# Gathering u by pair and v by token: two half-size gathers in place of one, and the sum over v in 32-column products

## The chip, the core and the metric

The kernel runs on one core of a Trainium2 chip, in float32 throughout. The metric is the device time of one execution in microseconds (us), median of several runs. Five engines work side by side: PE (TensorE, matrix products), DVE (VectorE), ACT (ScalarE), POOL (GpSimd), which here issues the indirect DMAs, and SP, which issues the plain loads. 16 DMA engines move the data.

## The reference

Two blocks are computed, one after the other, on 256 tokens of width 1024; the first block also carries 256 context tokens. The change touches one part of the first block, the expert layer:

```python
def peer_ffn(x, w_q, sub_keys, u_emb, v_emb):      # chunks of 128 tokens
    q = (xc @ w_q).reshape(128, 8, 2, 128)
    s = einsum('thid,hikd->thik', q, sub_keys)
    # top 16 of each half, top 16 of their 256 sums: eidx, top_s [128, 8, 16]
    gate = softmax(top_s, axis=-1)
    u = u_emb[eidx]
    hid = gelu(einsum('td,thkd->thk', xc, u))
    wgt = gate * hid
    return einsum('thk,thkd->td', wgt, v_emb[eidx])
```

Each token has 8 heads x 16 = 128 pairs (head, rank), and each pair names one of 16,384 experts. An expert has a row of u and a row of v, 1024 floats (4 KB) each. For each pair the token's vector is multiplied with the u row and summed (the dot), the result goes through gelu and the gate, and with this weight the v row is added to the token's output. The layer runs three times: over the 256 tokens in layer 0, over the 256 context tokens in layer 0, and over the 256 tokens in layer 1.

## The kernel before

Each run of the expert layer (here a gather stage; its name in the code is `peer00`, `peer01` or `peer10`) takes two tiles of 128 tokens, with the tokens on the partitions. A tile has 8 steps, one a head, so a stage has 16 steps of 16 pairs: 256 gathers `e`.

- `peer_sp` loads the query weights and keys. `peer_pe` makes the queries and then, step by step, the scores (line 1180).
- `route_dve` turns one step's scores into 16 expert numbers and 16 gates for every token. It is a generator: `peer_dve` runs one piece of it for step+1 after each dot of step, from the third on (`next(routing, None)`), and the rest at the end of the step. The tenth piece gives the numbers and the gates.
- `peer_pool` issues one indirect DMA for each pair (line 1334). Row t of it is the expert row that token t names, from a table `uv` in which an expert's u and v rows lie side by side: 128 rows of 8 KB, about 1 MB. They land in a ring of 8 slots in `big`. At a step's end `fetched_pool` makes POOL wait until the step's last gather has landed, since the expert numbers have only two buffers.
- DVE takes the dot of the u half with the tokens' vectors, which lie in PSUM (line 1300). ACT makes gelu of the one column in four instructions (lines 1222 to 1225). DVE spreads weight times gate on the diagonal of a 128 x 128 matrix (line 1309), and PE multiplies this diagonal with the v half in two products of 512 columns, which add up in PSUM over the tile's 128 pairs (line 1200). Each such float32 product stands in the profile as two records.
- A slot comes free when PE has summed its v half. After a tile DVE multiplies the sum with the modulation row and adds it to `h` (lines 1319 and 1324).

The second stage, `peer01`, has side work: `together` weaves `ahead_pe`, `ahead_act` and `ahead_dve` between the steps. They make projections of the next layer in 8 turns, each with 2 MB and 1.5 MB of weights that SP loads when PE has finished with the buffer, and results stored by ACT's queue. The main programs say by `yield` how far they are, from 0 to 256, and each side program's pieces come due as a share of that.

## Time and profile before

| | |
|---|---|
| runs, median (lowest to highest) | 4519.16 us (4517.67 to 4519.98) |
| profiled execution: time / span | 4520.76 us / 4519.5 us |
| PE busy / DVE busy / ACT busy / POOL busy | 3599.4 / 2209.3 / 1248.7 / 834.0 us |
| indirect gathers | 768, 805.36 MB in all |
| mean granted TensorE clock | 0.918 of full speed |

The span is the time from the first to the last instruction of the profiled execution, and the views of the trace count microseconds from its start. Busy time is the time in which an engine worked; it says nothing of what held the kernel up. For that one reads which wait ended last in each stage.

### The profile page before, as it was taken

To read this page: it belongs to the slowest core of one execution; us is meant where nothing else is said; L and a number is where in the kernel's file an instruction comes from. 1 tells how busy PE (TensorE), PEld (TensorE's weight loads), DVE (VectorE), ACT (ScalarE), POOL (GpSimd) and SP (SyncE) were. 2 spreads that over 40 slices of the span, in tenths; PEclk is the share of its full clock that TensorE was granted. 3 is DMA by queue.
4 is the path that set the end of the run, shared out by engine and by line. 5 is a ranking of instruction groups with operands and counts; after the bars stand their busy time and mean duration, and the time that the engine had idled before them with its cause. 6 is when DMAs were issued, how large, how long until landed. Compare 5 with 4: busy or idle time off the path is not lost.

```text
span 4519.5 us, 30080 instructions
## 1 busy us (share of the span) xinstructions
PE 3599.4 (80%) x9346; PEld 1688.1 (37%) x9346; DVE 2209.3 (49%) x4937; ACT 1248.7 (28%) x3913; POOL 834.0 (18%) x872
## 2 busy tenths in 40 slices
PE   7799998878777777679898897777777777787786
PEld 1144444544422222254444443343522222234343
DVE  0101520462577777536777775333377777622132
ACT  0010000331244444324444442021244444411111
POOL 0000100000233333213233332000133333300000
PEclk9899999989999999889999998988899899998898
DMA  7712222022689898869999997212689898942322
GB/s 268 264 56 75 56 75 79 21 75 74 274 363 384 361 382 364 341 224 385 401 401 389 404 392 271 93 63 94 238 365 384 362 382 363 380 157 75 115 80 93
DMA packets 283753, 1087.17 MB, mean 241 GB/s; under 512 B 17180, under 2 KB 73500, under 8 KB 184256
## 3 DMA queue, kind: packets, MB, share of 16 engines
q0 software_dynamic: 110592, 805.36, 43.7%
q1 hardware_dynamic: 169672, 274.65, 17.6%
q10 hardware_dynamic: 3328, 5.24, 0.3%
q8 instruction: 73, 1.20, 0.1%
q14 instruction: 88, 0.72, 0.0%
HBM read 1078.79 MB, written 6.40 MB: 240 GB/s over the span
## 4 chain that ended last, share of the span: by engine, by line
PE 52%; DMA 29%; DVE 11%; issue 3%; POOL 2%; ACT 1%; SPq 1%; DVEq 0%; POOLq 0%; ACTq 0%
DMA big<-in_uv,smallu 22%; PE ps L221 18%; PE ps L1200 13%; PE ps L477 6%; PE ps L415 4%; PE ps L1168 3%; DVE tmp L1300 3%; DMA w<-in_w_in 2%; DMA w<-in_w_mod 2%; PE ps L1069 2%; PE ps L489 2%; DMA w<-in_peer_wq 2%; POOL big L1334 2%; DVE xT L1309 1%; PE ps L1078 1%
## 5 line engine op out<-in xcount | busy, mean ns | idle before, releaser
L1200 PE MATMUL ps<-big,xT 128*128 128x512 f32 x3072 | 1534.3, 637 | 441.0 <-DVE xT L1309 439.6
L1300 DVE CUSTOM_DVE_ANT_0 tmp<-big,ps 128x1024 f32<-128x1024 f32 x768 | 934.5, 1217 | 507.8 <-DMA big<-in_uv,smallu 504.9
L1200 PEld LDWEIGHTS ps<-big,xT 128*128 128x128 f32 x3072 | 582.1, 200 | 1302.9 <-DVE xT L1309 770.7
L1334 POOL DMA_INDIRECT big<-in_uv,smallu x768 | 727.7, 948 | 1646.0 <-PE ps L1200 1097.7
L221 PE MATMUL ps<-w,xT 128*128 128x512 f32 x1600 | 697.6, 598 | 31.7 <-DMA w<-in_w_in 26.4
L1222 ACT ACTIVATE xT<-xT 128x1 f32<-128x1 f32 x768 | 155.7, 203 | 1163.3 <-DVE xT L1300 1156.2
L221 PEld LDWEIGHTS ps<-w,xT 128*128 128x128 f32 x1600 | 306.2, 192 | 418.1 <-issue 410.7
L1309 DVE TENSOR_SCALAR xT<-ident,xT 128x128 f32<-128x128 f32 x768 | 274.6, 363 | 140.0 <-ACT xT L1225 140.0
L1225 ACT ACTIVATE xT<-xT 128x1 f32<-128x1 f32 x768 | 297.2, 387 | 25.7
L477 PE MATMUL ps<-w,xT 128*128 128x512 f32 x576 | 259.1, 612 | 54.4 <-DMA w<-in_w_in 53.2
L1224 ACT ACTIVATE xT<-xT 128x1 f32<-128x1 f32 x768 | 226.1, 294 | 25.1
L1223 ACT ACTIVATE xT<-xT,small 128x1 f32<-128x1 f32 x768 | 226.1, 294 | 24.9
L1168 PE MATMUL ps<-tmp,w 128*128 128x256 f32 x768 | 178.6, 396 | 39.8 <-DMA w<-in_peer_wq 37.7
L221 PE MATMUL ps<-w,small 128*2 128x512 f32 x384 | 169.1, 597 | 31.9 <-DMA w<-in_w_mod 31.0
L477 PEld LDWEIGHTS ps<-w,xT 128*128 128x128 f32 x576 | 112.5, 197 | 197.8 <-issue 189.3
L1168 PEld LDWEIGHTS ps<-tmp,w 128*128 128x128 f32 x768 | 152.8, 200 | 64.4 <-DMA w<-in_peer_wq 38.9
L415 PE MATMUL ps<-xT,w 128*128 128x512 f32 x384 | 165.1, 592 | 0.7 <-ACT big L393 0.7
L231 PE MATMUL ps<-ident,merged 128*128 128x128 f32 x208 | 43.0, 395 | 122.4 <-DVE merged L282 49.3
L1069 PE MATMUL ps<-w,merged 128*128 128x512 f32 x256 | 130.2, 617 | 5.4 <-DVE tmp L1121 4.9
L518 DVE TENSOR_SCALAR tmp<-tmp 128x512 f32<-128x512 f32 x36 | 15.4, 427 | 235.4 <-ACT tmp L508 233.6
L253 ACT ACTIVATE tmp<-h 128x1024 f32<-128x1024 f32 x22 | 23.2, 1056 | 383.6 <-DVE big L332 199.2
L366 POOL TENSOR_TENSOR small<-small 128x32 f32<-128x32 f32 x8 | 43.3, 5415 | 464.2 <-DVE small L356 464.2
(207 smaller groups left out, 2610.2 us busy)
## 6 DMA issues: line engine op xcount, KB each, us to landing
w<-in_w_in SPq DMA_DIRECT2D x48, 2048.0 KB
w<-in_w_mod SPq DMA_DIRECT2D x24, 2048.0 KB
w<-in_w_in SPq DMA_DIRECT2D x48, 512.0 KB
w<-in_peer_wq SPq DMA_DIRECT2D x12, 2048.0 KB
w<-in_w_out SPq DMA_DIRECT2D x8, 2048.0 KB
big<-in_uv,smallu POOLq DMA_INDIRECT x768
bc<-mods SPq DMA_DIRECT2D x20, 512.0 KB, 7.0
w<-in_conv_out_w SPq DMA_DIRECT2D x4, 2048.0 KB
```

The costliest lines, as they stand in the source:

```text
L221: ins = pe.e.matmul(self.ps[0:rows, b, :], lhs(k, tile), self.wk(s, kc)[:, k, :], start=k == 0, stop=k == kc - 1)
L415: ins = pe.e.matmul(self.ps[:, 3 * s + g, 0:n], view[:, k, g, :], self.xT[:, k, 0:n], start=k == 0, stop=k == KC - 1)
L477: ins = pe.e.matmul(self.ps[:, self.gate_bank(n, product, c, i), :], self.lhs(k, tile), self.wk(s)[:, k, :], start=k == 0, stop=k == KC - 1)
L1069: ins = pe.e.matmul(self.ps[:, 6 + i, :], xT[:, k, i * P:(i + 1) * P], proj_w[:, k, :], start=k == 0, stop=k == KC - 1)
L1168: ins = pe.e.matmul(self.ps[:, 5 + i % 3, 0:256], self.wk(c % 2)[:, k, g * P:(g + 1) * P], p["xT"][:, k, :], start=k == 0, stop=k == KC - 1)
L1200: ins = pe.e.matmul(self.ps[:, 2 + half, :], p["diag"][:, e % RING, :], p["ring"][:, e % RING, D + half * BANK:D + (half + 1) * BANK], sta ...
L1223: act.inc(act.x.activation(g1, g1, ACT.Identity, scale=0.044715 * ROOT, bias=self.root_2_pi))
L1224: act.inc(act.x.activation(g2, g1, ACT.Tanh, scale=x))
L1225: act.inc(act.x.activation(wt, g2, ACT.Identity, scale=x, bias=x), name, "gelu", e)
L1300: dve.inc(dve.e.tensor_tensor_reduce(out=p["junk"][k % 2], in0=p["ring"][:, e % RING, 0:D], in1=p["xc"], scale=1.0, scalar=0.0, op0=ALU.mu ...
L1309: dve.inc(dve.e.tensor_scalar(p["diag"][:, e % RING, :], self.ident[:, :], p["wt"][u][:, c:c + 1], p["gates"][u][:, c:c + 1], ALU.mult, AL ...
L1334: ins = pool.e.indirect_dma_start(p["ring"][:, e % RING, :], None, self.d["uv"], bass.IndirectOffsetOnAxis(p["eidx"][step % 2][:, k:k + 1] ...
```

## The change

The table `uv` is split in two, `u` and `v`. A gather fetches 128 rows of 4 KB of one table, so a stage has 512 of them, each half as large. The ring in the same memory has 16 slots of half the size.

For u, a gather still belongs to one pair, with the tokens on the partitions. For v it belongs to one token, with that token's 128 pairs on the partitions: the expert numbers of a tile are turned on PE (`turn_experts`) and copied to `eidxT`. So v of a tile can be fetched only when all 8 steps of it are routed, and summed only when all 128 dots of it are done. `peer_order` sets one order for all engines: the 128 u gathers of tile 0; then v of tile 0 and u of tile 1 in turn; then the 128 v gathers of tile 1. They are called parts A, B and C here.

Gelu is made once a tile on 128 x 128 values: five instructions on DVE and one tanh on ACT (`gelu_dve`). PE turns the weights, and DVE writes them with stride 33 into two zeroed buffers of 2048 columns (`diag_dve`). Token 32j+m has there a block of 128 x 32 in which only column m is filled. Its product with the token's v rows adds the weighted sum of the 128 pairs to row m of the PSUM partitions 32j to 32j+31. Four tokens, one of each j, are taken in a group: 8 products of 512 columns. The numbers and gates of a whole tile are kept, so that `fetched_pool` is gone. A u slot comes free with its dot, a v slot with its group's products.

```diff
-RING, LAG = 8, 2
+RING, LAG = 16, 2
...
+    def peer_order(self):
+        order = [("u", e) for e in range(P)]
+        for i in range(P):
+            order += [("v", i), ("u", P + i)]
+        return order + [("v", P + i) for i in range(P)]
...
     def peer_pe(self, pe, l, stream):
...
-                pe.wait_ge(self.dve, name, "spread", e)
-                for half in range(2):
-                    ins = pe.e.matmul(self.ps[:, 2 + half, :], p["diag"][:, e % RING, :], p["ring"][:, e % RING, D + half * BANK:D + (half + 1) * BANK],
...
+            if n == 0:
+                turn_weights(tile)
+                pe.wait_ge(self.dve, name, "diag", tile)
+                if tile:
+                    pe.wait_ge(self.dve, name, "summed", 0)
+            if n % 4 == 3:
+                m, slots = n // 4, [self.v_slot[e - 3 + j] for j in range(4)]
                 for half in range(2):
+                    for j in range(4):
+                        if not half:
+                            pe.wait_ge(self.gathered[slots[j]], name, "v", e - 3 + j)
+                        ins = pe.e.matmul(self.ps[32 * j:32 * j + 32, 2 + half, :], p["diag"][j // 2][:, (j % 2) * D + 32 * m:(j % 2) * D + 32 * m + 32],
+                                          p["ring"][:, slots[j], half * BANK:(half + 1) * BANK], start=m == 0, stop=m == 31)
+                pe.inc(ins, name, "sum", e // 4)
...
     def route_dve(self, dve, l, name, p, step):
...
-        if step >= 2:
-            dve.wait_ge(self.pool, name, "fetched", step - 2)
-        dve.inc(dve.x.tensor_tensor(p["eidx"][u], row[:, 0:16], row[:, 16:32], ALU.add), name, "experts", step)
+        dve.inc(dve.x.tensor_tensor(p["eidxf"][tile][:, cols], row[:, 0:16], row[:, 16:32], ALU.add))
+        dve.inc(dve.x.tensor_copy(p["eidx"][tile][:, cols], p["eidxf"][tile][:, cols]), name, "experts", step)
...
+    def gelu_dve(self, dve, name, p, tile):
+
+        x, g1, g2 = p["hid"][tile], p["g1"], p["g2"]
+        dve.inc(dve.x.tensor_tensor(g1, x, x, ALU.mult))
+        dve.inc(dve.x.tensor_scalar(g1, g1, 0.044715 * ROOT, ROOT, ALU.mult, ALU.add))
+        dve.inc(dve.x.tensor_tensor(g1, g1, x, ALU.mult), name, "inner", tile)
+        dve.inc(dve.x.tensor_tensor(x, x, p["gates"][tile], ALU.mult))
+        dve.wait_ge(self.act, name, "tanh", tile)
+        dve.inc(dve.x.scalar_tensor_tensor(out=g2, in0=g2, scalar=1.0, in1=x, op0=ALU.add, op1=ALU.mult), name, "weights", tile)
...
     def peer_dve(self, dve, l, stream, ahead=False):
...
+            slot = self.u_slot[e]
+            dve.wait_ge(self.gathered[slot], name, "u", e)
...
+            dve.inc(dve.e.tensor_tensor_reduce(out=row, in0=row, in1=p["xc"], scale=1.0, scalar=0.0, op0=ALU.mult, op1=ALU.add,
+                                               accum_out=p["hid"][tile][:, e % P:e % P + 1]), name, "dot", e)
+            if k >= LAG:
+                next(routing, None)
+            if e % P == P - 1:
+                alone(routing)
+                self.gelu_dve(dve, name, p, tile)
+                self.diag_dve(dve, name, p, tile)
+                if tile:
+                    self.summed_dve(dve, name, p, 0, self.h[:, 2 * stream, :])
...
     def peer_pool(self, pool, l, stream):
...
+        for at, (kind, e) in enumerate(order):
+            tile, n, slot = e // P, e % P, at % RING
+            if at >= RING:
+                before, b = order[at - RING]
+                if before == "u":
+                    pool.wait_ge(self.dve, name, "dot", b)
+                else:
+                    pool.wait_ge(self.pe, name, "sum", b // 4)
+            if kind == "u":
+                if e % TOPK == 0:
+                    pool.wait_ge(self.dve, name, "experts", e // TOPK)
...
+                if n == 0:
+                    pool.wait_ge(self.dve, name, "eidxT", tile)
...
-    def fetched_pool(self, pool, name, step):
-
-        pool.wait_ge(self.gathered[(step * TOPK + TOPK - 1) % RING], name, "row", step * TOPK + TOPK - 1)
-        pool.inc(pool.e.nop(), name, "fetched", step)
...
-        together(self.peer_pe(pe, 0, 1), [(0, 256, self.ahead_pe(pe.beside()))])
+        together(self.peer_pe(pe, 0, 1), [(0, 512, self.ahead_pe(pe.beside()))])
```

The side work of the second stage is spread over the 512 places of the new order, a quarter of it over part A.

What stands on the engines changes as follows. On POOL, at the start of the first gather stage of the kernel before (`waits` names the counters that an instruction waits for; `gathered7` is the landing of ring slot 7):

```order
L1334 DMA big<-in_uv,smallu 128x2048 [waits dve_ops]
L1334 DMA big<-in_uv,smallu 128x2048 x7
L1334 DMA big<-in_uv,smallu 128x2048 [waits pe_ops] x8
L1334 DMA big<-in_uv,smallu 128x2048 [waits gathered7,pe_ops,dve_ops]
L1334 DMA big<-in_uv,smallu 128x2048 [waits pe_ops] x15
```

In the changed kernel POOL has at the end of part A and the start of part B of that stage (line 1392 is the new issue):

```order
L1392 DMA big<-in_u,xT 128x1024 x11
L1392 DMA big<-in_u,xT 128x1024 [waits dve_ops] x4
L1392 DMA big<-in_v,xT 128x1024 [waits dve_ops]
L1392 DMA big<-in_u,xT 128x1024 [waits dve_ops]
L1392 DMA big<-in_v,xT 128x1024
```

The wait for a landing is gone from POOL; in part A it waits for DVE alone, and the first u of tile 1 waits for numbers of the ninth step. Further on in part B:

```order
L1392 DMA big<-in_v,xT 128x1024 [waits pe_ops]
L1392 DMA big<-in_u,xT 128x1024 [waits dve_ops]
L1392 DMA big<-in_v,xT 128x1024
L1392 DMA big<-in_u,xT 128x1024 [waits dve_ops]
L1392 DMA big<-in_v,xT 128x1024
L1392 DMA big<-in_u,xT 128x1024 [waits dve_ops]
```

Here POOL waits for PE once in four v gathers, where before it waited for every slot. On DVE, the kernel before has in the middle of the first stage dots (ISA, line 1300, with the read of the accumulator behind) and spreads in turn:

```order
L1300 ISA tmp,xT<-big,ps 128x1024 [waits gathered5]
L1300 ISA xT 128x1
L1309 TENSOR_SCALAR xT<-ident,xT 128x128 [waits pe_ops]
L1300 ISA tmp,xT<-big,ps 128x1024 [waits dve_ops,gathered6]
```

In the changed kernel DVE has at the end of part A, behind the last dots of tile 0 (line 1360):

```order
L1360 ISA big,xT<-big,ps 128x1024 [waits gathered14]
L1360 ISA xT 128x1
L1360 ISA big,xT<-big,ps 128x1024 [waits gathered15]
L1360 ISA xT 128x1
L1303 TENSOR_TENSOR xT<-xT 128x128 [waits dve_ops]
L1304 TENSOR_SCALAR xT<-xT 128x128 [waits dve_ops]
L1305 TENSOR_TENSOR xT<-xT 128x128 [waits dve_ops]
L1306 TENSOR_TENSOR xT<-xT 128x128 [waits dve_ops]
L1308 SCALAR_TENSOR_TENSOR xT<-xT 128x128 [waits dve_ops,act_ops]
L1316 COPY tmp<-ps 128x2x32 [waits dve_ops,pe_ops]
L1316 COPY bc<-ps 128x2x32 [waits dve_ops]
L1348 COPY ps<-merged 128x512 [waits dve_ops] x2
```

The spreads are gone from between the dots, and the gelu of the tile stands in one piece between the tiles. On PE, the kernel before has at the start of the first stage's sums:

```order
L1200 MATMUL ps<-big,xT 128x512 [waits dve_ops]
L1200 MATMUL ps<-big,xT 128x512
L1200 MATMUL ps<-big,xT 128x512 [waits dve_ops]
```

The changed kernel has there, at the start of part B (1199 turns the expert numbers, 1203 the weights, 1194 makes scores):

```order
L1199 MATMUL ps<-ident,xT 128x128 [waits dve_ops]
L1194 MATMUL ps<-bc,bb 128x128 [waits dve_ops]
L1194 MATMUL ps<-bc,bb 128x128
L1203 MATMUL ps<-ident,xT 128x128 [waits dve_ops]
L1194 MATMUL ps<-bc,bb 128x128 [waits dve_ops]
L1194 MATMUL ps<-bc,bb 128x128
L1230 MATMUL ps<-big,tmp 32x512 [waits gathered0]
L1230 MATMUL ps<-big,tmp 32x512 [waits gathered2]
L1230 MATMUL ps<-big,bc 32x512 [waits gathered4]
L1230 MATMUL ps<-big,bc 32x512 [waits gathered6]
L1230 MATMUL ps<-big,tmp 32x512 x2
L1230 MATMUL ps<-big,bc 32x512 x2
```

The sums no longer wait for DVE, but for the landings of a group's four tokens, and each product fills 32 rows of the result.

## Rows read from the trace of the kernel before

**Rows 1.** Page, chain that ended last, by line.

```profile
DMA big<-in_uv,smallu 22%; PE ps L221 18%; PE ps L1200 13%; PE ps L477 6%; PE ps L415 4%; PE ps L1168 3%; DVE tmp L1300 3%; DMA w<-in_w_in 2%; DMA w<-in_w_mod 2%; PE ps L1069 2%; PE ps L489 2%; DMA w<-in_peer_wq 2%; POOL big L1334 2%; DVE xT L1309 1%; PE ps L1078 1%
```

**Rows 2.** Windows: stretch, its length, engines' busy us (instructions), PEclk, DMA share, GB/s.

```profile
1188.00:1900.00 712.00, 523.73 (x1080) 201.13 (x1080) 521.11 (x1324) 305.27 (x1053) 235.03 (x248) 0.92 0.90 366
2014.00:2766.00 752.00, 676.18 (x1714) 328.99 (x1712) 535.78 (x1362) 312.10 (x1067) 233.98 (x248) 0.96 0.98 388
3253.00:3965.00 712.00, 526.32 (x1080) 201.93 (x1080) 521.99 (x1325) 305.23 (x1052) 235.76 (x248) 0.92 0.90 366
5.00:200.00 195.00, 168.10 (x383) 31.29 (x384) 15.62 (x23) 0.00 (x0) 0.00 (x0) 1.00 0.75 268
```

**Rows 3.** Timeline: PE and DVE where the first gather stage begins and ends.

```profile
1187.03 0.61 PE L1180 MATMUL ps<-bc,bb 128*128 128x128 f32 x4
1899.90 1.42 DVE L1319 TENSOR_TENSOR tmp<-ps,bc 128x512 f32<-128x512 f32 x2 [4.08 <-PE ps L1200]
```

**Rows 4.** Groups by line, 1255 to 1900 us: busy us, mean ns | idle before.

```profile
L1200 PE MATMUL ps<-big,xT 128*128 128x512 f32 x920 | 465.5, 646 | 172.5 <-DVE xT L1309 172.2
L1300 DVE CUSTOM_DVE_ANT_0 tmp<-big,ps 128x1024 f32<-128x1024 f32 x228 | 277.5, 1218 | 145.4 <-DMA big<-in_uv,smallu 145.0
L1334 POOL DMA_INDIRECT big<-in_uv,smallu x224 | 212.0, 946 | 420.5 <-PE ps L1200 239.9 <-DMA big<-in_uv,smallu 152.4 <-issue 27.6
L1309 DVE TENSOR_SCALAR xT<-ident,xT 128x128 f32<-128x128 f32 x230 | 82.1, 363 | 11.4 <-ACT xT L1225 11.4
```

**Rows 5.** Waits, 1255 to 1900 us: total us, times, longest us.

```profile
POOL big L1334 <- DMA big<-in_uv,smallu: 152.4, 14, 12.3
```

**Rows 6.** Timeline: POOL at a step's start; first gather and first dot.

```profile
1397.06 0.94 POOL L1334 DMA_INDIRECT big<-in_uv,smallu  x1 [10.79 <-DMA big<-in_uv,smallu]
1398.30 0.94 POOL L1334 DMA_INDIRECT big<-in_uv,smallu  x1 [0.30 <-issue]
...
3205.42 1.05 POOL L1334 DMA_INDIRECT big<-in_uv,smallu  x1 [34.27 <-DVE xT L1276]
3211.03 1.22 DVE L1300 CUSTOM_DVE_ANT_0 tmp<-big,ps 128x1024 f32<-128x1024 f32 x1 [3.91 <-DMA big<-in_uv,smallu]
```

**Rows 7.** Timeline: DVE in the middle of a step, successive dots.

```profile
1233.00 1.22 DVE L1300 CUSTOM_DVE_ANT_0 tmp<-big,ps 128x1024 f32<-128x1024 f32 x1 [0.26 <-DMA big<-in_uv,smallu]
...
1237.98 1.22 DVE L1300 CUSTOM_DVE_ANT_0 tmp<-big,ps 128x1024 f32<-128x1024 f32 x1 [0.25 <-DMA big<-in_uv,smallu]
...
1240.46 1.22 DVE L1300 CUSTOM_DVE_ANT_0 tmp<-big,ps 128x1024 f32<-128x1024 f32 x1 [0.32 <-DMA big<-in_uv,smallu]
```

**Rows 8.** Timeline: DVE where thirteen gathers had already landed.

```profile
1189.27 0.30 DVE L1235 MAX8 xT<-ps 128x8 f32<-128x128 f32 x1
...
1212.25 1.21 DVE L1300 CUSTOM_DVE_ANT_0 tmp<-big,ps 128x1024 f32<-128x1024 f32 x1
1213.39 0.34 DVE L1309 TENSOR_SCALAR xT<-ident,xT 128x128 f32<-128x128 f32 x1
1213.65 1.21 DVE L1300 CUSTOM_DVE_ANT_0 tmp<-big,ps 128x1024 f32<-128x1024 f32 x1
...
1217.59 0.60 DVE L1309 TENSOR_SCALAR xT<-ident,xT 128x128 f32<-128x128 f32 x2
```

**Rows 9.** Timeline: PE, products of 64 rows, then of 128 rows.

```profile
860.62 1.13 PE L638 MATMUL ps<-w 64*128 64x512 f32 x4
...
883.08 2.85 PE L638 MATMUL ps<-w 64*128 64x512 f32 x12
...
1894.44 5.42 PE L1200 MATMUL ps<-big,xT 128*128 128x512 f32 x12 [0.44 <-DVE xT L1309]
```

**Rows 10.** Page: the second stage's side products; the gathers' DMA queue.

```profile
L1069 PE MATMUL ps<-w,merged 128*128 128x512 f32 x256 | 130.2, 617 | 5.4 <-DVE tmp L1121 4.9 <-ACT xT L1222 0.6
L1078 PE MATMUL ps<-merged,w 128*128 128x256 f32 x384 | 98.1, 385 | 0.0
q0 software_dynamic: 110592, 805.36, 43.7%
```

More of the change, by code:

```diff
@@ L1242, in route_dve @@
     def route_dve(self, dve, l, name, p, step):
-        u = step % 2
+        tile, cols = step // PEER_HEADS, slice(step % PEER_HEADS * TOPK, step % PEER_HEADS * TOPK + TOPK)
         dve.wait_ge(self.pe, name, "scores", step)
@@ new lines, in diag_dve, with summed_dve @@
+    def diag_dve(self, dve, name, p, tile):
+        dve.wait_ge(self.pe, name, "weights turned", tile)
+        if tile:
+            dve.wait_ge(self.pe, name, "sum", 31)
+        for a in range(2):
+            out = p["diag"][a].rearrange("p (j r) -> p j r", j=2)[:, :, 0:D:33]
+            dve.inc(dve.x.tensor_copy(out, p["turnedW"][:, 64 * a:64 * a + 64].rearrange("p (j m) -> p j m", j=2)))
+        dve.mark(name, "diag", tile)
+    def summed_dve(self, dve, name, p, tile, h):
+        t = self.merged[:, tile, :]
+        dve.wait_ge(self.row_in[0], "row", name, "gate")
+        dve.wait_ge(self.pe, name, "sum", 32 * tile + 31)
+        for half in range(2):
+            c = slice(half * BANK, (half + 1) * BANK)
+            dve.inc(dve.x.tensor_tensor(t[:, c], self.ps[:, 2 + half, :], self.bc[:, 0, c], ALU.mult))
+        dve.mark(name, "summed", tile)
+        for half in range(2):
+            c = slice(half * BANK, (half + 1) * BANK)
+            dve.inc(dve.x.tensor_tensor(h[:, c], h[:, c], t[:, c], ALU.add))
@@ L1283, in peer_dve @@
             dve.inc(dve.x.memset(self.bc[:, 5, BANK:BANK + SEQ + 2], 0.0))
+        for a in range(2):
+            dve.inc(dve.x.memset(p["diag"][a], 0.0))
         alone(self.route_dve(dve, l, name, p, 0))
-        for step in range(STEPS):
-            tile, head, u = step // PEER_HEADS, step % PEER_HEADS, step % 2
-            if not head:
+        routing = iter(())
+        for at, (kind, e) in enumerate(self.peer_order()):
+            yield at
+            if kind == "v":
+                continue
+            tile, step, k = e // P, e // TOPK, e % TOPK
+            if e % P == 0:
@@ L1312, in peer_dve @@
-            alone(routing)
-            if head == PEER_HEADS - 1:
-                dve.wait_ge(self.row_in[0], "row", name, "gate")
-                dve.wait_ge(self.pe, name, "sum", step * TOPK + TOPK - 1)
-                for half in range(2):
-                    c = slice(half * BANK, (half + 1) * BANK)
-                    t = p["junk"][1][:, c]
-                    dve.inc(dve.x.tensor_tensor(t, self.ps[:, 2 + half, :], self.bc[:, 0, c], ALU.mult))
-                dve.mark(name, "summed", tile)
-                for half in range(2):
-                    c = slice(half * BANK, (half + 1) * BANK)
-                    t, hh = p["junk"][1][:, c], self.h[:, tile + 2 * stream, c]
-                    dve.inc(dve.x.tensor_tensor(hh, hh, t, ALU.add))
+            if k == 0:
+                if step % PEER_HEADS == 7:
+                    dve.wait_ge(self.pe, name, "experts turned", tile)
+                    dve.inc(dve.x.tensor_copy(p["eidxT"][tile], p["turnedE"]), name, "eidxT", tile)
+                alone(routing)
+                routing = self.route_dve(dve, l, name, p, step + 1) if step + 1 < STEPS else iter(())
@@ L1326, in peer_pool @@
+            if e % P == P - 1:
+                alone(routing)
+                self.gelu_dve(dve, name, p, tile)
+                self.diag_dve(dve, name, p, tile)
+                if tile:
+                    self.summed_dve(dve, name, p, 0, self.h[:, 2 * stream, :])
+        self.summed_dve(dve, name, p, 1, self.h[:, 2 * stream + 1, :])
     def peer_pool(self, pool, l, stream):
         name, p = f"peer{l}{stream}", self.peer_views()
[L1328 to L1338 removed]
```

132 lines of the change are left out of this document (55 added, 77 removed).

## The prediction, as it stood before the changed kernel ran

> **What bounds the kernel now.** I read first the chain that ended last [rows 1]: the largest share, 22%, is the gathers' landing; PE's sum over v (line 1200) is 13%. Then the windows of the three gather stages [rows 2], from the end of the query products (1187.0 us) to the last sum (1899.9) [rows 3]. They take 712, 752 and 712 us, and the DMA engines are busy 0.90, 0.98 and 0.90 of them. No compute engine comes near that in need: DVE is busy 521 of 712 us.
>
> Inside a stage the groups by line show who waits [rows 4]: DVE's dots wait for landings (145 us), and POOL waits for PE's slots (240 us) and for a landing (152 us). The waits name that second one as 14 waits, one a step, up to 12.3 us long [rows 5]. It is `fetched_pool`: the queue runs dry once a step, POOL starts again, and the next gathers are 1.24 us apart at issue [rows 6]. Between these pauses the dots that wait for their row start at 1233.00, 1237.98 and 1240.46 [rows 7]: 7.46 us for three gathers, 2.49 us each. So a stage of 712 us is 256 x 2.49 = 637 us of transfer at its pace and some 75 us of pauses, 4.7 us a step. Transfer is the bound; the pauses are what could be won.
>
> **The change, part by part.** I cost parts A, B and C of the new order in a stage without side work, from the end of the query products.
>
> *Part A, 128 u gathers.* Here DVE has twice as many dots for each megabyte. What it needs is seen in the first step, where thirteen rows had landed already [rows 8]: from the first instruction of the routing (1189.27) to the spread behind the last dot (1217.59) are 28.3 us, with 13 dots, 12 spreads and one whole routing. A dot is 1.14 us (1212.25 to 1213.39), with its spread 1.40, so the routing is 28.3 - 13 x 1.14 - 12 x 0.26 = 10.4 us. One copy more, about 0.2 us, makes it 10.6. A step needs 16 x 1.14 + 10.6 = 28.8 us of DVE; its 16 gathers of 0.52 MB need at most 21 us of transfer. So DVE bounds part A, and the DMA engines idle a quarter of it. Three dots are made before the queries end, as now, which leaves 1.2 + 125 x 1.14 + 8 x 10.6 = 228.5 us.
>
> Numbers for the next step exist after a step's twelfth dot. Four dots and the gates follow, about 5 us. The first landing takes 5.6 us from the issue now (3205.42 to 3211.03 [rows 6]); with half the bytes 1.3 less, 4.3, and 0.3 us to start. That just fits; I allow 0.7 us of stall in seven steps, 5 us in all. Part A: 233.4 us.
>
> *The turn from A to B.* Gelu, the turning of the weights and their writing are about ten short dependent instructions, some 5 us. POOL meanwhile has 16 slots to fill, so the queue doesn't run dry: it hides the turn. It may issue the first v before, but waits with the first u of tile 1 for the ninth step's numbers, which come 5 us before A's last dot. So 383 gathers are left at A's end less 5 us.
>
> *Parts B and C.* DVE needs 1.14 + 10.6/16 = 1.8 us a pair in B, under the 2.6 of two gathers, and is hidden. POOL needs 1.24 us a gather [rows 6], near the transfer's time: a floor. The time of a 0.52 MB gather no row shows. By bytes alone it is half of 2.49, 1.245 us. The nearest rows with smaller pieces are the plain weight loads of 2 KB rows: 268 GB/s at a DMA share of 0.75, 357 GB/s at full share, against 366/0.90 = 407 for 8 KB rows [rows 2]. At that rate a gather is 1.47 us, the upper bound. The DMA time of one row, with 16 engines, is 0.092 us for 2 KB and 0.322 for 8 KB, on a line 0.169 for 4 KB: 4.7% more than half the 8 KB row. 1.245 x 1.047 = 1.30 us. I take 1.30.
>
> The ring limits less than before: when four v's are summed, about five to seven gathers are still under way, and POOL then issues at 1.24.
>
> PE: now 2 products = 4 records of 0.44 us a pair (12 in 5.42 us [rows 9]), so 1.77 us for a v. For 32-column products the trace has no row. If they run one after another it stays 1.77 us, more than 1.30, and PE would bound part C. The nearest row is line 638, products that use 64 of the 128 rows, two halves in turn: 12 records in 2.85 us where 12 full ones take 5.42 [rows 9]. So products on separate parts of the array overlap in float32 too, by two at least, and I take at most 0.9 us for a v: hidden.
>
> End: first landing 4.3 us after the issue at A's end less 5, then 382 x 1.30 = 496.6, then 3 us for the rest of the last group. The stage is 233.4 - 5 + 4.3 + 496.6 + 3 = 732 us, 20 more than 712. In words: 75 us of pauses are gone, the DMA's idle time in A costs about 66 (233 less the 128 x 1.30 = 166 of its transfers), and the dearer rows about 28 (512 x 0.055).
>
> *The second stage.* Its loads and stores use the pauses of now: 752 us, only 40 more than the others. Their own DMA time is the busy 0.98 x 752 = 737 us less 248 gathers at 2.58 (0.90 x 712/248) = 96 us, or less 248 at 2.49 = 119; I take 108. Two of the eight turns come due in part A and one more load starts there, where the engines idle; about 0.65, 70 us, must lie beside gathers that fill the queue. DVE's side work and the loads between gathers in part A: 6 + 5 us. 732 + 11 + 70 = 813 us, 61 more.
>
> ACT loses its four instructions a pair; what waited for it, the spread, is gone. The clearing of the two buffers lies before the first scores, where DVE waits.
>
> Sum: 20 + 61 + 20 = +101 us on the profiled execution's 4519.5 us of span (its time is 4520.8, the median of the runs 4519.2: 1.6 apart). **4620 us**, +2.2%.
>
> A rule of the Trainium skill speaks against this change beyond that: DMA: Bandwidth & Descriptors (Rules for kernel authors) wants 1 MiB or more in a DMA, and its fit (Anatomy of one DMA) is 2.0 us + bytes/436 GB/s, by which two halves cost 6.4 us and the whole 4.4. This case's 2.49 us for a whole lies below 4.4, so most of the fixed part is hidden when gathers queue; by the fit alone a stage would be 512 x 3.2 = 1638 us, which no row supports.
>
> **Rivals.**
>
> *PE serial in part C.* 32-column products don't overlap: part C takes 32 groups x 7.1 us = 227 us instead of 166, and the 7 us in which PE waits for the second gelu count too: +68 a stage. In the second, two turns of side products fall in C, 2 x (32 x 0.43 + 48 x 0.21) = 48 us [rows 10], +89. Together +225: 4845 us. Against it is line 638; for it, that those were row halves, not column quarters. 0.10.
>
> *Halves cost more than rows.* A smaller gather loses more at its ends, or the queue runs low at each step of A: 1.36 us a gather and 2 us more stall a step: 1149 x 0.06 + 21 x 2 = +111, 4731 us. This is the direction of the skill's rule on size. For it are 110,592 packets for 768 gathers [rows 10], 144 each of which 16 are not data: that part doubles. 0.18.
>
> *Not slower: bytes alone count.* 4 KB rows go at the 8 KB rate, so POOL's 1.243 us sets the pace, and A has no stall: 228.5 - 0.7 + 382 x 1.243 + 3 = 705.6 us, 6 less than now. The second stage: with 0.65 of the 96 us 774 (+22), in sum 4528 us; with 0.65 of the 40 us that this traffic adds now 738 (-14), in sum 4492. It decides from about 1.25 us a gather down. For it is that POOL and byte rate happen to agree; against it are the 2 KB loads. 0.13, half of it faster.
>
> *The forecast:* 1.27 to 1.33 us a gather: 4585 to 4655. 0.55. The rest, 0.04, is anything else, slower more likely.
>
> **How the numbers follow.** The time is the likeliest case's, 4620. The range leaves out the serial PE (0.10) and the faster half of the last rival with a bit beyond: 4525 to 4740. Two in a thousand, 9 us, is what a measurement can tell from no change. Slower: 0.55 + 0.18 + 0.10 and a little; same and faster share the last rival, and I add a little for what I overlook: faster 0.09, same 0.08, slower 0.83.
>
> **What would show it.** Part A: some 29 us between the first dots of successive steps, DVE over 0.9 busy, DMA share near 0.75. Parts B and C: DMA share 0.97 or more, POOL's starts 1.30 apart, waiting for DVE or PE now and then. A v group's 16 records within 4 us. Wrong would be: POOL never waiting in B (pace 1.24), PE busy through all of C (serial), landings late at each step of A, or the second stage less than 30 us over its 752.

## The result and the profile after

The changed kernel takes 4588.3 us (median of four runs, 4585.2 to 4591.8) against 4518.4 for the kernel before: ratio 1.0157, 95% interval 1.0140 to 1.0175. It is slower by 1.6%. The profiled execution has a span of 4586.9 us, 67.4 more than before.

The page of the changed kernel: DMA share and rate in 40 slices, the gathers' queue, and the chain by line.

```profile
DMA  7712212022578999868899998312577999951322
GB/s 265 261 55 74 74 56 81 17 78 102 224 291 336 409 409 408 336 241 304 320 403 404 401 402 315 110 62 92 194 274 300 409 409 409 409 187 68 119 78 92
q0 software_dynamic: 221184, 805.40, 44.8%
PE ps L224 18%; POOL big L1392 12%; DMA big<-in_u,xT 10%; DMA big<-in_v,xT 8%; DVE big L1360 7%; PE ps L480 6%; PE ps L418 4%; PE ps L1178 3%; DMA w<-in_w_in 2%; DMA w<-in_w_mod 2%; PE ps L1230 2%; PE ps L492 2%; DMA w<-in_peer_wq 1%; DVE small L734 1%; PE ps L234 1%
```

The 768 gathers of 8 KB rows are now 1536 of 4 KB rows: 221,184 packets where [rows 10] had 110,592, with the same 805.4 MB. In the first and third gather stage (slices 11 to 17 and 29 to 36) the rate begins low, at 224 to 336 and 194 to 300 GB/s, and then stands at 408 to 409. In the chain PE's sum over v has fallen from 13% [rows 1] to 2%, DVE's dot has risen from 3% to 7%, and POOL's issue of gathers from 2% to 12%.

Windows of the changed kernel, same columns as [rows 2]: parts A, B and C of the three stages, then the stages whole.

```profile
1177.00:1419.00 242.00, 9.27 (x32) 6.78 (x30) 221.67 (x556) 3.47 (x17) 109.45 (x117) 0.51 0.66 248
1419.00:1751.00 332.00, 211.59 (x541) 35.24 (x542) 227.84 (x532) 3.11 (x15) 244.06 (x260) 0.78 1.02 407
1751.00:1914.00 163.00, 138.86 (x513) 25.24 (x512) 4.81 (x13) 0.31 (x1) 113.12 (x121) 0.99 1.00 399
2016.00:2261.00 245.00, 63.60 (x198) 39.79 (x197) 224.48 (x564) 6.24 (x23) 110.48 (x118) 0.62 0.80 288
2261.00:2637.00 376.00, 276.36 (x862) 92.26 (x860) 236.01 (x555) 8.83 (x27) 244.10 (x259) 0.85 1.03 402
2637.00:2816.00 179.00, 160.80 (x663) 48.40 (x663) 8.83 (x21) 3.40 (x7) 112.55 (x120) 0.98 1.02 398
...
1177.00:1914.00 737.00, 359.71 (x1085) 67.26 (x1084) 454.32 (x1098) 6.89 (x33) 466.63 (x496) 0.74 0.90 353
2016.00:2816.00 800.00, 500.77 (x1721) 180.45 (x1720) 469.33 (x1138) 18.47 (x57) 467.13 (x496) 0.81 0.96 366
3293.00:4029.00 736.00, 357.90 (x1090) 67.80 (x1088) 454.29 (x1099) 7.00 (x33) 467.02 (x496) 0.74 0.90 354
```

Part A has DVE busy 221.7 of 242 us and the DMA engines 0.66. PE has 9 us of work there, and its granted clock is 0.51, its lower level. In B and C the DMA engines are at 1.00 to 1.03, with 398 to 407 GB/s (a share over 1 means that the times of packets on one engine overlap), and PE is far from full in B. POOL isn't: the 260 issues of B, at 1.24 us [rows 6], are 322 of 332 us, so it stands close to being the bound itself. The whole stage reads 0.90 and 353 GB/s beside 0.90 and 366 of before: nearly the same DMA time, but idle for another reason, in one piece at the front and no longer once a step.

The timeline of the changed kernel: the first gather of the first stage, the last of the query products and the scores behind them, and the first instruction after the last sum.

```profile
1139.33 1.18 POOL L1392 DMA_INDIRECT big<-in_u,xT  x1 [34.33 <-DVE xT L1297]
...
1176.69 0.61 PE L1194 MATMUL ps<-bc,bb 128*128 128x128 f32 x4
...
1915.30 1.42 DVE L1326 TENSOR_TENSOR merged<-ps,bc 128x512 f32<-128x512 f32 x2 [158.58 <-PE ps L1230]
```

From the queries' end to the last sum are 1915.30 - 1176.69 = 738.6 us, where [rows 3] give 712.9; the second stage (2019.01 to 2818.94) takes 799.9 for 752.2, the third (3293.19 to 4028.81) 735.6 for 712.2. That is +25.7, +47.7 and +23.4, +96.8 in sum. Against it stands something that the prediction did not have: from a stage's first gather to the end of the query products pass 37.4 us, and before 1187.03 - 1140.43 = 46.6 [rows 3] (POOL's first gather of the kernel before is at 1140.43 in its timeline). The other two stages show 40.3 for 50.3 and 37.5 for 46.5. This stretch, from the first gather to the end of the query products, is called the approach below. The three approaches give back 28.1 us, and 96.8 - 28.1 = 68.7 us is the span's 67.4 to within a little over one.

DVE in part A of the changed kernel, all its waits from 1178 to 1418 us (us, times, longest), and below them its dots in the middle of B, the first two and the last of seven in a row.

```profile
DVE big L1360 <- DMA big<-in_u,xT: 11.1, 14, 1.3
```

```profile
1734.55 1.22 DVE L1360 CUSTOM_DVE_ANT_0 big<-big,ps 128x1024 f32<-128x1024 f32 x1 [1.34 <-DMA big<-in_u,xT]
...
1737.14 1.22 DVE L1360 CUSTOM_DVE_ANT_0 big<-big,ps 128x1024 f32<-128x1024 f32 x1 [1.35 <-DMA big<-in_u,xT]
...
1749.83 1.22 DVE L1360 CUSTOM_DVE_ANT_0 big<-big,ps 128x1024 f32<-128x1024 f32 x1 [1.34 <-DMA big<-in_u,xT]
```

The dots wait 11.1 us for landings in all of part A. These seven in B wait 1.3 us each, and six pairs take 1749.83 - 1734.55 = 15.28 us, so a gather of 0.52 MB takes 1.273 us; [rows 7] gave 2.49 for one of 1.05 MB.

PE at the end of a group of four v's in C of the changed kernel.

```profile
1893.08 0.62 PE L1230 MATMUL ps<-big,bc 128*32 128x512 f32 x1 [0.23 <-DMA big<-in_v,xT]
1893.09 0.62 PE L1230 MATMUL ps<-big,tmp 128*32 128x512 f32 x2
1893.10 1.03 PE L1230 MATMUL ps<-big,bc 128*32 128x512 f32 x2
1893.54 0.60 PE L1230 MATMUL ps<-big,tmp 128*32 128x512 f32 x2
1893.56 1.00 PE L1230 MATMUL ps<-big,bc 128*32 128x512 f32 x2
1894.36 0.62 PE L1230 MATMUL ps<-big,tmp 128*32 128x512 f32 x1
1894.39 0.59 PE L1230 MATMUL ps<-big,bc 128*32 128x512 f32 x1
1894.82 0.59 PE L1230 MATMUL ps<-big,tmp 128*32 128x512 f32 x1
1895.64 1.04 PE L1230 MATMUL ps<-big,tmp 128*32 128x512 f32 x2 [0.23 <-DMA big<-in_v,xT]
```

Each line is one to three records. They overlap: between 1893.08 and 1895.4 PE ends twelve of them, the work of three v's, and then waits for the next v with 0.23 us idle.

### The profile page after: what moved, and what is told of

The parts are those of the page before. It is cut to its first block, busy times and chain, and to the rows that moved or that the text cites. A ratio compares the mean times of both kernels' runs of the same rounds, so it can differ in the third digit from the quotient of the medians.

```text
span 4586.9 us, 26483 instructions
## 1 busy us (share of the span) xinstructions
PE 3084.0 (67%) x9358; PEld 1262.5 (28%) x9358; DVE 2020.0 (44%) x4271; ACT 353.5 (8%) x847; POOL 1552.6 (34%) x1640
## 3 DMA queue, kind: packets, MB, share of 16 engines
q0 software_dynamic: 221184, 805.40, 44.8%
## 4 chain that ended last, share of the span: by engine, by line
PE 37%; DMA 24%; DVE 19%; POOL 12%; issue 5%; ACT 1%; SPq 1%; DVEq 0%; ACTq 0%; POOLq 0%
PE ps L224 18%; POOL big L1392 12%; DMA big<-in_u,xT 10%; DMA big<-in_v,xT 8%; DVE big L1360 7%; PE ps L480 6%; PE ps L418 4%; PE ps L1178 3%; DMA w<-in_w_in 2%; DMA w<-in_w_mod 2%; PE ps L1230 2%; PE ps L492 2%; DMA w<-in_peer_wq 1%; DVE small L734 1%; PE ps L234 1%
## 5 line engine op out<-in xcount | busy, mean ns | idle before, releaser
L1360 DVE CUSTOM_DVE_ANT_0 big<-big,ps 128x1024 f32<-128x1024 f32 x768 | 928.1, 1216 | 361.9 <-DMA big<-in_u,xT 360.9
L1392 POOL DMA_INDIRECT big<-in_u,xT x768 | 722.1, 940 | 687.3 <-DVE xT L1298 356.3
L1230 PE MATMUL ps<-big,bc 128*32 128x512 f32 x1536 | 683.4, 726 | 293.8 <-DMA big<-in_v,xT 293.7
L1392 POOL DMA_INDIRECT big<-in_v,xT x768 | 724.1, 943 | 317.2 <-issue 205.8
L1230 PE MATMUL ps<-big,tmp 128*32 128x512 f32 x1536 | 630.7, 705 | 104.6 <-DMA big<-in_v,xT 99.9
L1230 PEld LDWEIGHTS ps<-big,bc 128*32 128x32 f32 x1536 | 110.4, 120 | 806.3 <-DMA big<-in_v,xT 650.2
L1194 PE MATMUL ps<-bc,bb 128*128 128x128 f32 x192 | 43.7, 365 | 397.3 <-DVE smallu L1262 320.7
L1230 PEld LDWEIGHTS ps<-big,tmp 128*32 128x32 f32 x1536 | 80.2, 116 | 341.0 <-DMA big<-in_v,xT 299.9
L606 POOL COPY w<-big 128x512 f32<-128x512 f32 x32 | 18.5, 614 | 427.4 <-DVE merged L532 336.8
L1194 PEld LDWEIGHTS ps<-bc,bb 128*128 128x128 f32 x192 | 35.7, 253 | 422.9 <-DVE smallu L1262 205.4
```

Source lines behind the costliest of these rows:

```text
L1194: ins = pe.e.matmul(p["score"][:, i * P:(i + 1) * P], p["qT"][:, tile, g, :], p["keys"][:, g * P:(g + 1) * P], start=True, stop=True)
L1230: ins = pe.e.matmul(self.ps[32 * j:32 * j + 32, 2 + half, :], p["diag"][j // 2][:, (j % 2) * D + 32 * m:(j % 2) * D + 32 * m + 32], p["rin ...
L1360: dve.inc(dve.e.tensor_tensor_reduce(out=row, in0=row, in1=p["xc"], scale=1.0, scalar=0.0, op0=ALU.mult, op1=ALU.add, accum_out=p["hid"][t ...
L1392: ins = pool.e.indirect_dma_start(p["ring"][:, slot, :], None, table, bass.IndirectOffsetOnAxis(index, 0))
```

## The experiments

Times are medians of four runs, except where a single run is named; the kernel before took 4513 to 4517 us beside them.

**What the pauses were worth.** `e1` is the kernel before with numbers for all 16 steps kept (16 buffers), so that POOL never waits for its own gathers.

```
-        if step >= 2:
-            dve.wait_ge(self.pool, name, "fetched", step - 2)
-        dve.inc(dve.x.tensor_tensor(p["eidx"][u], ...
+        dve.inc(dve.x.tensor_tensor(p["eidx"][step], ...
...
-                if k == TOPK - 1:
-                    self.fetched_pool(pool, name, step)
```

> The kernel before, with expert numbers of all 16 steps kept, so that POOL no longer waits at a step's end for the last landing. My theory (a stage without side work is 256 transfers of 2.49 us and 75 us of pauses, which this wait makes): the first and third stage fall from 712 to about 645 us, the second by 0 to 15 us, since its side transfers filled the pauses; in all 4370 to 4395 us. Rival (the pauses come from POOL waiting for free slots and for late numbers, and the landing wait only shows them): under 30 us a stage are won, 4460 us or more.

Measured 4388.9 us, ratio 0.9724 (0.9708 to 0.9741); the first stage takes 1830.50 - 1182.88 = 647.6 us.

Waits of POOL in the first stage of this kernel (us, times, longest).

```profile
POOL big L1332 <- PE ps L1200: 331.7, 215, 11.5
POOL big L1332 <- DVE smallu L1272: 48.8, 15, 3.4
```

The wait for the landing [rows 5] is gone. PE's slots hold POOL, and once a step the next step's numbers, up to 3.4 us. 65 us in the first stage and 64 in the third (648.0 for 712.2) came from a few columns of memory: there the pauses are a cost that needs no new order of the gathers. The second stage takes 752.1 us for 752.2: its side transfers had filled the pauses already.

**Halving the gathers alone.** `e2` is the kernel before with each gather as two, from tables u and v apart.

```
-                ins = pool.e.indirect_dma_start(p["ring"][:, e % RING, :], None, self.d["uv"], ...
+                ins = pool.e.indirect_dma_start(p["ring"][:, e % RING, 0:D], None, self.d["u"], index)
+                self.gathered[e % RING].inc(ins)
+                ins = pool.e.indirect_dma_start(p["ring"][:, e % RING, D:2 * D], None, self.d["v"], index)
```

> The kernel before, each 8 KB gather split in two gathers of 4 KB rows, one from u and one from v, into the same slot; order, waits and arithmetic as before. My theory (4 KB rows cost 1.28 to 1.30 us a gather against 1.245, and small gather packets leave the plain weight loads beside them a larger share, which is why the queries of the changed kernel end some 9 us earlier after the first gather): a step is 16 x 2.58 + 4 to 5 us, so 728 to 740 us from the queries' end to the last sum in the first stage (712 before), and 37 us instead of 47 from the first gather to the queries' end; in all about 4530 to 4565 us. Rival A (half-size gathers cost nothing): 4490 to 4510, by the earlier queries alone. Rival B (the earlier queries of the changed kernel come from POOL issuing its first 8 MB over 20 us in place of 10): this kernel also issues 8 MB over 20 us, so it can't tell that from the packet size; it can only rule out both if the queries end as late as before.

Measured 4576.1 us, ratio 1.0143 (1.0126 to 1.0160), 11 us above the expected band. The first gather is at 1141.18 and the queries end at 1178.88: 37.7 us, close to the changed kernel's 37.4, so splitting the gathers is enough to shorten the approach. The stage behind it is 743.6 us for 712.9, 4 us above the 740 expected at most.

**Why the queries end earlier.** `e6` is the kernel before, with POOL held for about 1 us between the first eight gathers of a stage.

```
+                elif e:
+                    n = self.pause.inc(pool.e.tensor_tensor(s, ..., ALU.pow))
+                    pool.e.wait_ge(self.pause.sem, n)
```

> The kernel before, with one short GpSimd operation of about 1.2 us between the first eight gathers of each stage, so that its first 8 MB are issued over about 20 us as in the changed kernel, but in 8 KB rows. Theory P (the queries end earlier in the changed kernel because packets of 4 KB in the gather queue leave the 2 KB packets of the weight loads a larger share): the queries still end about 46 us after the first gather. Theory I (they end earlier because POOL issues the same bytes over a longer time): about 37 us. Either way the kernel as a whole stays within 4490 and 4525 us.

POOL and PE in this kernel: the first gathers, and the scores behind the queries.

```profile
1141.75 1.17 POOL L1339 DMA_INDIRECT big<-in_uv,smallu  x1 [34.26 <-DVE xT L1277]
1142.95 1.05 POOL L1337 TENSOR_TENSOR small<-small 128x4 f32<-128x4 f32 x1
1144.29 1.01 POOL L1339 DMA_INDIRECT big<-in_uv,smallu  x1 [0.29 <-POOL small L1337]
...
1188.38 0.61 PE L1181 MATMUL ps<-bc,bb 128*128 128x128 f32 x4
```

The gathers start 2.4 us apart for 1.24, and the queries still end 46.6 us after the first (1188.38 - 1141.75); 4515.6 us in a single run, as before. In the second and third stage the approach is 47.2 us for 50.3 and 43.5 for 46.5, so there the rate of issue gives 3 us of the 9 to 10, and in the first stage nothing. What differs for the rest is the size of a packet (one row of a gather or a load): the query weights come in 2 KB pieces on another queue, and they finish sooner beside 4 KB pieces than beside 8 KB ones. The packets show it directly. The last piece of the query weights starts 39.7 us after the first gather in the kernel before, when the gathers' queue has moved 8.4 MB, and 31.5 us after it in the changed kernel, beside 5.1 MB. The Trainium skill (DMA: Bandwidth & Descriptors, Queues, rings and completion order) says that each engine takes the queues in turn and drains one packet, typically of 9 to 17 descriptors, before it switches. If its packets hold as many rows in both kernels, smaller rows on the one queue leave the other a larger share; the runs agree with that, but none shows what such a packet holds.

**Part A without its dots.** `e3` is the changed kernel with tile 0's dots over 64 of the 1024 columns; it leaves out the rest of that product.

```
+            n = 64 if e < P else D
-            dve.inc(dve.e.tensor_tensor_reduce(out=row, in0=row, in1=p["xc"], scale=1.0,
+            dve.inc(dve.e.tensor_tensor_reduce(out=row[:, 0:n], in0=row[:, 0:n], in1=p["xc"][:, 0:n], scale=1.0,
```

> The changed kernel, with the dots of each first tile made over 64 of 1024 columns (15/16 of that product is left out); every transfer, wait and order stays. My theory (DVE's dots and routing bound part A): DVE's need of a step falls from 29 to about 14 us, and part A is then bounded by its 16 transfers and the latency of the numbers, 21 to 24 us a step in place of 30.2: part A 175 to 195 us in place of 242, the kernel 140 to 200 us faster, 4390 to 4450. Rival (part A is held by the chain from numbers to issue to landing, whatever DVE's dots cost): less than 60 us in all.

Window of part A of this kernel.

```profile
1177.00:1350.00 173.00, 8.84 (x29) 6.53 (x29) 100.74 (x540) 3.20 (x16) 105.93 (x113) 0.51 0.89 333
```

4409.7 us in a single run, inside the expected band. DVE is busy 100.7 of 173 us, the DMA share is 0.89 instead of 0.66, and tile 0's last dot comes at 1354 us and not at 1418. DVE's dots bound part A, and without them the kernel is 179 us shorter (62, 49 and 62 us in the three stages).

**Products that can't overlap.** `e4` is the changed kernel with the four products of a group all in rows 0 to 31 of the sum, so that the sum comes out as another one.

```
-                        ins = pe.e.matmul(self.ps[32 * j:32 * j + 32, 2 + half, :], ...
+                        ins = pe.e.matmul(self.ps[0:32, 2 + half, :], ...
```

> The changed kernel, with all four products of a group sent to the same 32 rows of the result (the output of the sum over v is then another one); counts, sizes, waits stay. My theory (products of different 32-column parts overlap, which hides PE in parts B and C): now they can't overlap, a v takes 1.77 us of PE, part C grows from 164 to about 230 us in the first and third stage and by 80 to 90 in the second, in all about +200 us, 4770 to 4830. Rival (they hardly overlapped before, and PE wasn't the bound): within 20 us of 4588.

PE in this kernel: four records in 1.88 us, one after another; then the window of C.

```profile
1852.10 1.88 PE L1230 MATMUL ps<-big,bc 128*32 128x512 f32 x4
1853.81 1.88 PE L1230 MATMUL ps<-big,tmp 128*32 128x512 f32 x4
```

```profile
1750.00:1920.00 170.00, 167.06 (x390) 42.85 (x391) 6.63 (x15) 0.31 (x1) 98.05 (x106) 1.00 0.92 324
```

4824.9 us in a single run, 237 more than the changed kernel. PE is busy 167 of 170 us and the DMA share falls to 0.92. So the overlap of 32-column products is what keeps PE out of the way. The prediction's rival had +225, nearly the same sum, but not by its parts: the stages grow by 60, 112 and 65 us for 68, 89 and 68, and the prediction does not show how its 89 comes about.

**Routing earlier.** `e5` is the changed kernel with two pieces of routing a dot, so that the next step's numbers are ready sooner (ACT's exponential for the gates moves forward with it); `e7` does the same to `e1`; `e8` is `e1` with split gathers.

```
                 next(routing, None)
+                next(routing, None)
```

> The changed kernel, with two pieces of the next step's routing after each dot in place of one, so that a step's numbers exist after its seventh dot and not its twelfth. My theory (in part A POOL starts each step late because the numbers are late, which costs DVE about 11 us of waiting for landings, and at A's end POOL is held by the ninth step's numbers): the waits of 11 us go, the queue is full when B begins, 15 to 20 us a stage are won, 4530 to 4550 us in all; a step of part A still takes about 29 us, DVE's own need. Rival (late numbers cost nothing beside DVE's need): 4580 us or more.

> The kernel before without the landing wait on POOL, and with the routing two pieces at a time. Theory (without the pause a stage is 256 transfers of 2.49 us = 637 us and some 11 us at its ends and where POOL waits for late numbers): the numbers' part goes, 3 to 8 us a stage, 4365 to 4382 us. Rival (POOL's waits for numbers in the run without the pause are only the first of the chain and cost nothing): 4385 to 4392 us as without it.

> The kernel before without the landing wait, each gather split in two of 4 KB rows. It has the changed kernel's gathers and the old order of work. Theory (the halves cost 1.28 us a gather when the queue is full, against 1.245, and the queries end 9 us earlier): 512 x 1.28 = 655 + 8 us a stage against 648, less 9; 4385 to 4410 us in all. Then nearly all of the changed kernel's loss against it, some 190 us, is part A and the second stage's loads. Rival (halves are dear even in a full queue, 1.32 us or more, and most of the change's loss comes from them): 4430 us or more.

The theory missed in all three: 4645.7 us (ratio 1.0289, 1.0271 to 1.0306), 4450.5 (0.9864, 0.9847 to 0.9880) and 4541.4 (1.0069, 1.0049 to 1.0089). The first and third lie in the open bands of their rivals, but `e5` is 57 us slower than the changed kernel, which its rival doesn't explain either, and `e7` lies in no band. In `e5` part A did become shorter, 230 us for 242 (1180.00 to the gelu at 1410.09), and no dot waits for a landing in it; but B and C took 542 us for 496.

Windows of B: the changed kernel and `e5`; then `e1` and `e7` from 1200 to 1810 us, and `e8`.

```profile
1467.00:1734.00 267.00, 171.17 (x435) 27.54 (x435) 184.46 (x435) 2.40 (x12) 195.40 (x207) 0.78 1.03 409
```

```profile
1455.00:1763.00 308.00, 183.22 (x453) 29.52 (x453) 187.03 (x446) 2.40 (x12) 203.77 (x216) 0.75 0.96 368
```

```profile
1200.00:1810.00 610.00, 474.19 (x1019) 177.39 (x1017) 491.77 (x1258) 287.13 (x991) 229.12 (x241) 0.99 1.00 413
```

```profile
1200.00:1810.00 610.00, 452.31 (x970) 181.52 (x969) 473.95 (x1223) 275.13 (x944) 213.63 (x228) 0.95 0.97 391
```

```profile
1400.00:1750.00 350.00, 250.83 (x506) 99.28 (x504) 250.62 (x643) 141.75 (x489) 226.43 (x240) 0.89 0.96 362
```

The same gathers move 368 GB/s in `e5` where they moved 409, at a DMA share of 0.96 for 1.03; `e7` has 391 for 413. In `e8` 362 GB/s make 1.45 us of a gather of 0.52 MB. The view of DMA in 40 slices of `e5`'s stretch, 7.6 us each, shows that the rate is lost in bursts:

```profile
DMA  7999899997999899997999799998999899997999
GB/s 244 387 404 412 292 343 408 412 405 235 361 414 409 316 334 415 408 409 257 391 414 410 276 335 412 410 404 253 366 416 409 304 339 418 409 394 240 397 413 408
```

It falls to 235 to 316 GB/s about every 34 us and is back at 404 to 418 between; in the deepest dips the engines are busy 0.7 to 0.8 of the time, so that part of the loss is idle time and not only long packets. In the records of single packets a 4 KB packet takes 159 ns at the median; 2.8% of them, nearly all in these bursts, take over 1.3 times that, the longest 1.7 us. POOL's starts show the same period:

```profile
1558.00 0.94 POOL L1393 DMA_INDIRECT big<-in_v,xT  x1 [4.36 <-remote]
...
1592.12 0.93 POOL L1393 DMA_INDIRECT big<-in_v,xT  x1 [4.61 <-remote]
```

Each 24 gathers (34.1 us) POOL stands still for over 4 us; `remote` means that the profile finds no instruction or transfer that released it. By the count of packets each burst begins with the gather that POOL issued first after such a break, about 12 us later, when its packets come up; in `e7`, `e8` and part A of the changed kernel too. The kernel before has them as well, once a step: POOL starts again at 1397.06 [rows 6], and long packets come from about 1409 on. From 1200 to 1810 us 2.8% of its packets take over 1.3 times their median of 309 ns, which is 15 us a DMA engine, against 1.1% and 7 us in `e1`. By this estimate some 8 us of what the prediction counts as pauses in a stage are such bursts. The routing comes once in 32 gathers here, so its instructions are not what each burst answers to. Two ideas of the cause remained, and each got a test.

**Fewer gathers outstanding.** `e9`, `e10` and `e11` are `e5`, `e8` and `e7`, where POOL waits for the landing of the gather six, six (three pairs) and four before.

```
+            if at >= 6:
+                pool.wait_ge(self.gathered[(at - 6) % RING], name, *order[at - 6])
```

> The changed kernel with two pieces of routing a dot (as in the run whose routing came early, 4645.7 us), and POOL may issue a gather only once the gather six before it has landed. In that run the pure stretches moved 364 to 368 GB/s where the changed kernel moves 407 to 409, and packets of the gathers' queue grew from 159 ns to several hundred in bursts. Theory Q (the bursts come from many gathers outstanding when POOL runs ahead: 16 slots, so up to 16 of them): with at most six outstanding the bursts go, the second phase is back at 400 GB/s or more, and the time is 4540 to 4595 us. Rival D (the bursts come from VectorE's denser work or from the routing's data, not from the queue's length): the time stays at 4635 to 4655. Rival L (six are too few to keep the queue full, since a gather takes about 8.9 to 11 us from issue to landing and one starts every 1.27 us): the pace falls to about 9 us / 6 = 1.5 us a gather, and the time rises to 4700 us or more.

> The kernel before without its pause and with split gathers (4541.4 us), and POOL may issue a pair only once the pair three before it has landed, so at most six 4 KB-row gathers are outstanding instead of up to 16. Theory Q (long packets come from a long queue): its pure stages go from 360 to 373 GB/s up to 400 or more, and the time is 4385 to 4440 us. Rival D (other causes): 4530 to 4550, as without the limit. Rival L (six too few to fill the queue): 4600 or more.

> The kernel before without its pause and with two pieces of routing a dot (4450.5 us, against 4388.9 without the early routing), and POOL may issue a gather of 1 MB only once the gather four before it has landed. Theory Q: back to 4385 to 4400 us, with 415 GB/s or more in the pure stages (378 to 395 without the limit). Rival D: 4440 to 4460. Rival L: the landing of one gather 11 us after its issue over four outstanding, 2.8 us a gather instead of 2.5: 4500 or more.

4653.2 us (ratio 1.0304, 1.0287 to 1.0321), 4569.6 (1.0115, 1.0098 to 1.0132) and 4463.6 (0.9874, 0.9848 to 0.9899). From 1400 to 1750 us they move 368, 362 and 394 GB/s, where `e5`, `e8` and `e7` move 366, 362 and 390. A shorter queue cures nothing, so Theory Q falls. Rival L does too: the limits cost 7 us in `e9`, 28 in `e10` and 13 in `e11`. The band of Rival D held in `e9`, missed `e11` by 4 us and `e10` by 20. What it names as the cause, VectorE's denser work, was not varied by itself in any run.

**A break by itself.** `e12` is `e1`, with POOL held for 3.2 us before the 14th gather of each step.

```
+                if k == 13:
+                    for _ in range(3):
+                        n = self.pause.inc(pool.e.tensor_tensor(s, ..., ALU.pow))
+                        pool.e.wait_ge(self.pause.sem, n)
```

> The kernel before without its pause (4388.9 us), and POOL raises four columns to a power three times (about 1.05 us each, 3.2 us in all) before the 14th gather of each of the 48 steps. With its ordinary wait of up to 2.4 us for the sums that is a break of about 5.5 us in the issues, after which POOL catches up; up to eight gathers of 1 MB are outstanding, about 20 us of work for the DMA engines. In the kernels that lost rate (routing early, split gathers, and those with a limit on the gathers outstanding, which did not help) each burst of long packets begins exactly with the gather that POOL issued first after a break of 2.5 to 5 us, although the earlier gathers were still moving. Theory C (the break itself, followed by issues that catch up, makes the long packets): bursts that begin with the 14th gather of a step, under 405 GB/s in the pure stretches, and 4425 to 4465 us (the early routing cost 61 us over 48 steps, 1.3 us a step). Rival H (the break is hidden behind the queue, and the bursts had another cause, such as VectorE's denser work): 4384 to 4396, no bursts there.

POOL in this kernel at such a place, and the windows of `e12` in the first stage and in the second.

```profile
1387.58 0.94 POOL L1338 DMA_INDIRECT big<-in_uv,smallu  x1 [0.78 <-PE ps L1201]
1394.00 0.94 POOL L1338 DMA_INDIRECT big<-in_uv,smallu  x1 [5.49 <-PE ps L1201]
1395.72 0.94 POOL L1338 DMA_INDIRECT big<-in_uv,smallu  x1 [0.78 <-PE ps L1201]
```

```profile
1200.00:1810.00 610.00, 476.11 (x1020) 178.69 (x1020) 494.16 (x1269) 288.25 (x994) 275.99 (x286) 0.98 1.00 413
2020.00:2600.00 580.00, 499.51 (x1276) 240.27 (x1277) 400.48 (x1040) 233.97 (x798) 214.95 (x224) 0.94 0.99 389
```

4408.7 us, ratio 0.9756 (0.9739 to 0.9772). The break of 5.5 us is there, and the first stage keeps 413 GB/s, as in `e1`, with hardly more long packets (1.3% for 1.1%; `e7` has 3.4%): Theory C falls too. The time, 20 us over `e1`, lies in neither band. The first and third stage take 647.5 and 647.8 us, as in `e1`; the second, where side transfers share the engines, takes 770.0 for 752.1 (389 GB/s in its window, 397 in that of `e1`). What makes the bursts stays open.

## Why the prediction was right, step by step

The forecast was 4620 us, and the case it rested on came: slower, by 70 us where 101 were expected. Its steps:

- **Part A bound by DVE.** Right, and shown by `e3`. 242.1 us (1176.69 to 1418.8) for 233.4. Less the waits for landings DVE needed 231.0 for 228.5. The stalls were mis-sized: 11.1 us in 14 waits for 4.9. "That just fits" did not hold: early in each step dots wait for late rows, as at 1205.07 (1.16 us). The sign "DMA share near 0.75" did not come, it was 0.66; the prediction's own 166 us of transfer in 233 would have been 0.71.
- **The turn.** Gelu and the weights' turn take 1418.90 to 1421.75, 3 us for 5, and are hidden, since B's DMA share is 1.02.
- **1.30 us a gather.** The steady pace is 1.273; with the ends and C at 399 GB/s the two parts took 496.5 us for 498.9. Shown by the trace. It is only 0.03 above POOL's 1.24. The fear that halves cost more did not come true here, but it does in `e2` and `e8`: in `e8` the stage moves 362 GB/s. So the price of a half is not a constant of its size, and that the estimate from 2 KB rows fitted B is partly luck.
- **PE.** Overlap as taken from line 638, by four and not only by two; `e4` shows what its lack would cost.
- **The second stage.** +47.7 us for +61. It is 61.3 us longer than the first, where 81 were forecast. Its part A takes 242.4 us (2019.01 to the gelu at 2261.39), as in the first stage: the 11 us for DVE's side work and the loads did not come. There the DMA share is 0.80 for 0.66, so 0.14 x 245 = 34 us of side transfers found room, about the 38 that were taken (0.35 x 108); the rest cost B and C 61 us for 70.
- **Not foreseen: 28 us before the stages.** The sum began at the end of the query products and took their time as fixed. It is not: the weight loads share the engines with the gathers already under way. `e2` has the gain without the rest of the change, `e6` shows that it is not the rate of issue. With it the forecast would have been 4592.

The three stages' sum was right to 4 us (+97 for +101), and 28 of the 32 us missed are this one term. That the sum is so close is partly luck: the first and third stage came out 6 and 3 us above their +20, and the second 13 below its +61.

In a stage without side work the change buys the 75 us of pauses with part A's idle DMA engines, 242 us at 0.66, 82 us. `e1` gets the first without the second, and is 2.8% faster than before: 4388.9 us, 199 less than the changed kernel.

## What to carry to other kernels

When a transfer-bound loop shows its queue dry once a period, look first for what makes the issuer wait; keeping more index buffers removed 65 us of 712 here (and nothing where other transfers had filled the pauses), while a new order of the work brought in a stretch where another engine is the bound. Two orders with the same DMA share can idle for different reasons, so price every part by its own bound. And start the sum before the first gather, not behind the last load: here the two queues that ran side by side changed each other's times.

## What the runs showed of the hardware that was not expected

- Loads on one queue finish sooner beside smaller packets on another: in the first stage the query products end 37.3 to 38.1 us after the first gather with 4 KB rows (the changed kernel, `e2`, `e5`, `e8`; 39.5 in `e9`), and 46.5 to 46.7 with 8 KB rows (the kernel before, `e1`, `e7`, `e12`). Issues 2.4 us apart for 1.24 leave 46.6 in the first stage and take 3 us off in the other two (`e6`).
- Float32 products on four separate groups of 32 columns overlap: twelve records, three v's, end in 2.3 us, under 0.8 us a v, and a v costs 4 x 0.43 = 1.72 us when all four use the same group (`e4`).
- Gathers from POOL's queue can show bursts of long packets, some 10 us long and once in 16 to 24 gathers, that take their rate from 409 to about 365 GB/s with 4 KB rows (`e5`, `e8`) and from 413 to 391 with 8 KB rows (`e7`). The bursts follow a break in POOL's issues, yet a break alone doesn't make one (`e12`), and neither fewer gathers outstanding (`e9` to `e11`) nor, in `e5`, the period of the routing explains it. `e5` lost 57 us beside the changed kernel, `e7` 62 and `e8` 152 beside `e1`, of which the plain price of halves explains 43 (768 x (2 x 1.273 - 2.49)). The cause is open.
